# Mask and relative-position bias: from identity matmuls on TensorE to float32 additions in PSUM on VectorE

## The reference

```python
# layer 0, FoX: 16 heads of 128
s = einsum('bqhd,bkhd->bhqk', q, k) * scale
s = s + c[:, :, q0:kl, None] - c[:, :, None, :kl]      # forget-gate prefix sums
s = where(mask, s, -inf); p = softmax(s)
out = einsum('bhqk,bkhd->bqhd', p, v)

# layer 1, differential: 8 heads, two 128-wide q/k maps, 256-wide values
s = einsum('bqhmd,bkhmd->bhmqk', q, k) * scale
s = s + table[t5_bucket(qpos - kpos)]                  # bias by distance, constant from 128 on
s = where(mask, s, -inf); p = softmax(s)
a = p[:, :, 0] - lam * p[:, :, 1]
out = einsum('bhqk,bkhe->bqhe', a, v)                  # then per-head RMSNorm and gain
```

## Time and profile before

| | |
|---|---|
| time, median of 3 runs | 3136.53 us (3135.52 to 3137.95) |
| profiled execution, its own time | 3144.5 us |
| its span on the slowest core (core 4) | 3142.9 us |
| spans of the 8 cores | 3125.1 to 3142.9 us |
| mean granted TensorE clock, each core | 0.982 to 0.984 |
| busy: TensorE, ScalarE, VectorE, GpSimd | 94%, 37%, 33%, 4% |
| fox attention, units 0 to 6; unit 7 | 161 to 1183 us; 1183 to 1246 |
| first epilogue; layer 1's first projections | to about 1530; to 1666 |
| differential attention, units 0 to 6; unit 7 | 1666 to 2818; 2818 to 2890 |

### The profile page before, as it was taken

How to read it: one execution, slowest core, us unless ns; L and a number is a source line. 1 busy time by engine, 2 the same in 40 slices (tenths; PEclk the granted TensorE clock), 3 DMA queues, 4 the chain that set the end, 5 groups by cost and what they waited for, 6 DMA issues and landing times.

```text
span 3142.9 us, 63295 instructions; the slowest of 8 cores (3125.1 to 3142.9 us)
## 1 busy us (share of the span) xinstructions
PE 2968.9 (94%) x22516; PEld 2026.0 (64%) x22516; DVE 1027.2 (33%) x2722; ACT 1178.2 (37%) x2720; POOL 117.2 (4%) x239
## 2 busy tenths in 40 slices
PE   5999999999999996989599999999999999987998
PEld 2758686777768583434266867777777777665443
DVE  0122222222222222454213343434343333335455
ACT  0144554545454447222103333434343333245111
POOL 1000000000000000000000000000000000000000
PEclk9999999999999999999799999999999999999999
DMA  9222111112111119678621111111111111043565
GB/s 151 41 38 45 37 37 35 37 33 48 36 36 33 36 20 167 178 197 210 107 41 35 33 36 31 36 29 29 31 35 35 35 35 33 20 75 92 168 187 172
DMA packets 172112, 212.91 MB, mean 68 GB/s; under 512 B 105344, under 2 KB 150176, under 8 KB 155296
## 3 DMA queue, kind: packets, MB, share of 16 engines
q0 software_dynamic: 22944, 92.41, 17.6%
q1 hardware_dynamic: 148864, 116.47, 13.8%
HBM read 224.19 MB, written 51.90 MB: 88 GB/s over the span
## 4 chain that ended last, share of the span: by engine, by line
PE 84%; DMA 6%; DVE 3%; ACT 3%; issue 2%; SPq 1%; POOL 0%; DVEq 0%; ACTq 0%; POOLq 0%
PE pb L470 29%; PE pb L448 27%; PE pb L622 12%; PE pb L753 8%; PE pb L592 7%; DMA B<-M 3%; PE pb L595 2%; DMA W<-w_in 1%; ACT M L609 1%; DVE E L784 1%; DVE E L782 1%; ACT M L773 1%; DMA escr<-M 1%; ACT M L790 1%; SPq L791 1%
## 5 line engine op out<-in xcount | busy, mean ns | idle before, releaser
L609 ACT ACTIVATE M<-pb,L 128x256 bf16<-128x256 f32 (+1 forms) x1152 | 508.2, 460 | 468.0 <-PE pb L592 345.9
L613 ACT ACTIVATE M<-pb 128x256 bf16<-128x256 f32 (+1 forms) x1152 | 418.9, 371 | 680.4 <-PE pb L592 423.4
L448 PE MATMUL pb<-B,W 128*128 128x512 bf16 x2048 | 513.8, 380 | 35.5 <-ACT A L457 34.5
L448 PE MATMUL pb<-A,W 128*128 128x512 bf16 x2048 | 520.1, 382 | 21.4 <-DMA A<-x_t 21.4
L470 PE MATMUL pb<-W,A 128*128 128x256 bf16 x4096 | 524.3, 274 | 12.5 <-DMA W<-w_in 11.1
L470 PE MATMUL pb<-W,B 128*128 128x256 bf16 x4096 | 517.3, 273 | 0.0
L470 PEld LDWEIGHTS pb<-W,A 128*128 128x128 bf16 x4096 | 399.0, 98 | 57.1 <-issue 13.7
L622 PE MATMUL pb<-A,M 128*128 128x257 bf16 x2176 | 421.8, 274 | 12.3 <-DVE rin L656 6.7
L470 PEld LDWEIGHTS pb<-W,B 128*128 128x128 bf16 x4096 | 396.8, 98 | 45.2
L622 PE MATMUL pb<-B,M 128*128 128x129 bf16 x2176 | 307.4, 221 | 8.8 <-ACT M L609 4.0
L592 PE MATMUL pb<-B 128*128 128x256 bf16 (+1 forms) x1152 | 302.0, 267 | 13.7 <-ACT M L609 13.7
(11 more groups left out here) (87 smaller groups left out, 1854.0 us busy)
## 6 DMA issues: line engine op xcount, KB each, us to landing
W<-w_in POOLq DMA_DIRECT2D x61, 1024.0 KB, 8.5
gd<-M SPq DMA_DIRECT2D x128, 128.0 KB, 1.8
E<-x SPq DMA_DIRECT2D x16, 1024.0 KB, 6.6
x1d<-E SPq DMA_DIRECT2D x16, 1024.0 KB, 4.9
E<-x1d SPq DMA_DIRECT2D x16, 1024.0 KB, 6.4
y<-E SPq DMA_DIRECT2D x16, 1024.0 KB, 4.1
A<-w_out POOLq DMA_DIRECT2D x4, 2048.0 KB, 35.5
B<-w_out POOLq DMA_DIRECT2D x4, 2048.0 KB, 35.2
```

The source lines that it names most:

```text
L448: ins = e.matmul(pb[bk][:, :], lhsT=W[slot][:, kc, m * 128:(m + 1) * 128], rhs=Xbuf[:, kc, tc * 512:(tc + 1) * 512], start=(kc == 0), stop ...
L609: P.op("act", lambda e: e.activation(out=Pt[s][:, 0:w], in_=src, func=AF.Exp, bias=bsel[:, m, j, 2 * I:2 * I + 1], scale=SCALE), reads=rPB ...
L613: P.op("act", lambda e: e.activation(out=Pt[s][:, 0:w], in_=src, func=AF.Exp, scale=SCALE), reads=rPB(bank), writes=r_Pt(s, 0, w))
```

## The change

The identity, its table and its matmuls go. `nmask` and the bias table `Bt` are float32, the two bias blocks of a head side by side (distance 0, then distance 1). `qk` records a single score matmul, and for a diagonal tile one `tensor_tensor` on VectorE that adds the table to the score bank in place; the exponential then reads the bank. That is 32 additions in a fox unit (128 columns) and 46 in a differential one (30 of 128 columns, 16 of 256, j = 2I taking both bias blocks at once). In `setup_head_b` three VectorE operations a head take the place of six.

```diff
-        ident = sb("ident", [128, 128], BF16)
         tri_bf = sb("tri_bf", [128, 128], BF16)
-        nmask_bf = sb("nmask_bf", [128, 128], BF16)
+        nmask = sb("nmask", [128, 128], F32)
...
-                Bt = L[:, 0:4096].rearrange("p (h k l q) -> p h k l q", h=8, k=2, l=2)
+                Bt = L[:, 0:4096].bitcast(F32).rearrange("p (h w) -> p h w", h=8)
...
-                P.op("dve", lambda e: e.tensor_tensor(out=etmp[:, 0, :], in0=etmp[:, 0, :], in1=nmask_bf[:], op=ALU.add),
-                     reads=r0 + rS("nmask_bf"), writes=r0)
-                for k, rk in ((0, r0), (1, r1)):
-                    base = (h * 4 + k * 2) * 128
-                    P.op("dve", lambda e, k=k: e.tensor_copy(out=Bt[:, h, k, 0, :], in_=etmp[:, k, :]),
-                         reads=rk, writes=rL(base, base + 128))
-                    P.op("dve", lambda e, k=k: e.tensor_tensor(out=Bt[:, h, k, 1, :], in0=etmp[:, k, :], in1=Bt[:, h, k, 0, :], op=ALU.subtract),
-                         reads=rk + rL(base, base + 128), writes=rL(base + 128, base + 256))
+                P.op("dve", lambda e: e.tensor_tensor(out=Bt[:, h, 0:128], in0=etmp[:, 0, :], in1=nmask[:], op=ALU.add),
+                     reads=r0 + rS("nmask"), writes=rL(h * 512, h * 512 + 256))
+                P.op("dve", lambda e: e.tensor_copy(out=Bt[:, h, 128:256], in_=etmp[:, 1, :]), reads=r1, writes=rL(h * 512 + 256, h * 512 + 512))
...
-                    extra = []
-                    for k in range(nblk):
-                        d = i0 + k - j
-                        if fox and d == 0:
-                            extra.append((k, nmask_bf[:], rS("nmask_bf")))
-                        elif (not fox) and d in (0, 1):
-                            for l in range(2):
-                                base = (u * 4 + d * 2 + l) * 128
-                                extra.append((k, Bt[:, u, d, l, :], rL(base, base + 128)))
-                    def g(e):
-                        ins = e.matmul(pb[bank][:, 0:w], lhsT=o.k[:, m, j * 128:(j + 1) * 128], rhs=o.q[:, m, q0:q0 + w],
-                                       start=True, stop=(len(extra) == 0))
-                        for n, (k, rhs, _) in enumerate(extra):
-                            ins = e.matmul(pb[bank][:, k * 128:(k + 1) * 128], lhsT=ident[:], rhs=rhs, start=False, stop=(n == len(extra) - 1))
-                        return ins
...
+                    P.op("pe", lambda e: e.matmul(pb[bank][:, 0:w], lhsT=o.k[:, m, j * 128:(j + 1) * 128], rhs=o.q[:, m, q0:q0 + w],
+                                                  start=True, stop=True),
+                         reads=o.rk(m, j * 128, (j + 1) * 128) + o.rq(m, q0, q0 + w), writes=rPB(bank), sig=True)
+                    if fox:
+                        if j < 2 * I:
+                            return
+                        hi, add, r_add = 128, nmask[:], rS("nmask")
+                    else:
+                        if j < 2 * I - 1:
+                            return
+                        d0 = 0 if j >= 2 * I else 1
+                        hi = 256 if j == 2 * I else 128
+                        add = Bt[:, u, d0 * 128:d0 * 128 + hi]
+                        r_add = rL(u * 512 + d0 * 256, u * 512 + d0 * 256 + 2 * hi)
+                    P.op("dve", lambda e: e.tensor_tensor(out=pb[bank][:, 0:hi], in0=pb[bank][:, 0:hi], in1=add, op=ALU.add),
+                         reads=r_add, writes=rPB(bank))
```

More of the change, by code:

```diff
@@ L241, in build_program @@
         r_xres = [rng("E", 4096 + k * 4096, 8192 + k * 4096) for k in range(2)]
-        P.dma("pool", "c0", lambda e: e.dma_start(out=ident[:], in_=consts[:, 0:128]), writes=rS("ident"))
         P.dma("pool", "c1", lambda e: e.dma_start(out=tri_bf[:], in_=consts[:, 128:256]), writes=rS("tri_bf"))
         P.op("pool", lambda e: e.memset(lnst[:, 10:12], -0.5), writes=rS("lnst", 10, 12))
-        P.op("dve", lambda e: e.tensor_scalar(out=nmask_bf[:], in0=tri_bf[:], scalar1=-1.0, scalar2=BIG, op0=ALU.add, op1=ALU.mult),
-             reads=rS("tri_bf"), writes=rS("nmask_bf"))
+        P.op("dve", lambda e: e.tensor_scalar(out=nmask[:], in0=tri_bf[:], scalar1=-1.0, scalar2=BIG, op0=ALU.add, op1=ALU.mult),
+             reads=rS("tri_bf"), writes=rS("nmask"))
         wtile = {"next": 0}
```

## The result

| | before | after |
|---|---|---|
| time, median of 4 runs each | 3137.2 us (3135.5 to 3141.1) | 3214.6 us (3210.6 to 3219.9) |
| ratio | | 1.0246, 95% interval 1.0228 to 1.0264 |
| slowest core's span in the profiled execution | 3142.9 us (core 4) | 3214.1 us (core 0) |
| mean granted clock, each core | 0.982 to 0.984 | 0.968 to 0.970 |
| fox stage, first score matmul to last value matmul | 1081.8 us | 1096.6 us |

What follows compares the result with a forecast made beforehand. TensorE, busy 94% of the span, was taken as the bound, with VectorE's runs deciding the new waits. -62 + 42 + 41 + 4 + 25 + 15 + 30 = +95 us on 3136.5 gave 3232, range 3172 to 3282.

Steps and rivals of the forecast that it cites:

- A: Differential unit changes: first additions stand behind closing, GpSimd and output step; 6.9 us six times, 0.9 at unit 0, 42.
- B: Differential blocks 0 and 1 behind a unit's start: waits of 2.1, 2.2 and 1.6 us, seven times, 41 us.
- Removed: 1,248 identity matmuls gone; 1,092 in units 0 to 6 at 57 ns save 62 us, unit 7's count nothing.
- C: Tail of differential unit 6, without projections and with two banks: four diagonal groups at about 0.9 us, 4 us.
- D: Differential unit 7, where VectorE's runs cover three times as many tiles: waits at entry and in its blocks, 25 us.
- E: Fox layer: unit changes 0.8 us longer seven times (6), unit 7 (6), tail and collisions (3), together 15 us.
- tail and collisions: Small remaining fox losses outside the unit changes and unit 7, put at 3 us.
- F: Granted clock halved behind new waits: differential changes 6 x 2, fox 6 x 1.5, unit 7 5, blocks 0 and 1 4; 30 us.
- Waits without the clock: Rival: 2 us waits leave the clock up, unit 7's four banks hide half its losses; +45, 3182 us, chance 0.24.
- Hidden, faster: Rival: every addition gets VectorE within the 1.2 us slack per tile, only -62 remains; 3074 us, chance 0.04.
- Deeper: Rival: PSUM additions 60 ns longer, half clock at more waits, TensorE setting unit 7; +30, 3262 us, chance 0.14.
- Even: Rival: new waits and saving cancel, runs delaying only each front's first wait; within 6 us of 3137, chance 0.03.

Runs made afterwards that it cites:

- e1_none: The changed kernel with its VectorE additions left out, so no mask and no bias at all; ratio to before 0.9816.
- e4_late: The changed kernel, with the output step of a unit's last block not flushed at the unit change but deferred five iterations; 3202.75 us, ratio to before 1.0195.
- e6_unit7: The changed kernel with identity matmuls instead of VectorE additions in unit 7 of both layers; 3187.3 and 3187.6 us.
- e5_hybrid: The changed kernel with VectorE additions only in blocks where VectorE is free, identity matmuls elsewhere, unit 7 included; ratio to before 0.9898.
- e7_both: The kernel before with all identity matmuls kept, plus the changed kernel's 624 VectorE additions, of zeros; ratio to before 1.0372.
- e2_fox_only: The changed kernel with VectorE additions in the fox layer only, identity matmuls in the differential layer; ratio to before 1.0019.

## Why the forecast held, and where its terms were off

The mechanism is the one forecast: TensorE waits at each front of diagonal tiles behind a closing or an output step, in units 0 to 5 nothing above 0.21 us behind tile 17, and clock beside it. In units 1 to 5 a differential unit takes some 170.3 us against 157.7 in e1_none (distance of first score matmuls): 12.6, where A, B and the clock made 14.8. The two largest misses have opposite signs, the saving 7 us too large and B 15 us too large, so that the total is nearer than its terms.

| term | forecast | measured |
|---|---|---|
| removed | -62 | -55 (e1_none, stages) |
| differential layer: A 42, B 41, C 4, D 25, clock 12 + 4 + 3 | 131 | 113 |
| fox: E 15, clock 9 + 2 | 26 | 27 |
| sum | 95 | 84 in the stages; 77 in the medians |

**Removed** was 7 us too large, and not by its price: 56 ns an identity is what differential unit 0 and the fox units of e1_none show, against 57. The term left out that TensorE, coming sooner, meets the closing of map 0 at five changes (1.06 each) and at unit 7 (5.02 for 4.44). The Trainium skill's figure for such a stream (TensorE: Matmul & The Clock Gate, Back-to-back issue gap), 81 ns, would make it 88 us, an estimate; e1_none, 55 in the stages and 58 with 13 on either side in the time, speaks against it.

**A** held: 6.68 to 7.03 at five changes against 6.9, 5.81 at unit 6, and 0.74 at unit 0 against 0.9: 40.3. e4_late shows that the run ahead of the additions makes it.

**B** was the largest error in size: 41 forecast, 25.6 measured. Its three waits were to be 2.1, 2.2 and 1.6; they are 1.57, 1.47 and 1.01, 4.1 a unit against 5.9. The chain from VectorE free to matmul was right (1.11 us against 1.1). What failed is "Map 1 of block 0 is closed from 4.85 (its last value matmul)", and the tile times beside it. The accumulator of the first 128 queries is complete one iteration before, and its closing starts at 1842.06, 0.39 ahead of the last value matmul at 1842.45; it lasts 3.45 and not 3.1; and without its wait tile 8 would have come 2.60 behind that value matmul (1846.62 - 1.57 - 1842.45), where the forecast had 6.98 - 4.85 = 2.13. From 3.1 + 1.1 - 2.1 = 2.1 it became -0.4 + 3.45 + 1.1 - 2.6 = 1.6. And "seven times" was wrong for unit 6: more than one projection piece lies in each iteration there, tiles come later, and the waits of B are 0.63 and 0.68. Units 0 to 5 make 24.3, unit 6 makes 1.3.

**C** held: eleven waits of 0.18 to 1.21 in unit 6's tail, 4.5 together, where e1_none has four of 1.2 together: 3.3 against 4. **D** held: 27 by e6_unit7, of which some is clock (25, and about 3 of the 5 for unit 7). TensorE's first wait there, 4.44 in the earlier trace rows, became 7.03; 4.4 + 2.3 was forecast. Read singly, A 40.3, B 25.6, C 3.3, D 27 and the clock 14 (below) make 110; from them go the 7.3 that e1_none itself waits at the five changes (1.06 and 0.40 each), and 3.0 come on, by which unit 7 of e6_unit7 is longer than e1_none's. That leaves some 7 of the layer's 113 unplaced, about 1 a unit.

**E** was right in its sum, and its parts were not. Change waits are 2.48 against 2.5, and unit 7 is 6.2 against 6. But e6_unit7's fox stage, with identities in unit 7, is still 20.5 us over e1_none's: 4 are the changes (2.48 for 1.82 at five), 6 the clock, and some 10 are small losses at diagonals. In unit 4, whose clock stays up, they are five, of 0.18 to 0.27 us, all in or next to an iteration without a projection piece, as between two score matmuls at 325.93 and 327.15 in unit 1, 1.22 us where before has 1.09. The forecast had "tail and collisions: 3". The clock paid part back: 4 drops at six changes, since unit 6's wait is only 1.61 and one of 2.48 dropped nothing; 6 us instead of 9. e5_hybrid has 188 of these additions and no longer waits at a change than before, and its stage is 9.5 us over e1_none's, of which its 36 remaining identities are 2: the small losses without the large ones.

**F** was half right. Every differential change drops the clock. At the first it is back at about 1840, 3.8 us behind the end of the wait, at the others 4.2 to 5.4 us behind it; half of that is lost, 1.9 to 2.7 each and 14 together, against 12. No wait of B does: the 4 us for them did not come. The rival *Waits without the clock* (3182) falls with these rows, and it left out half of D, which e6_unit7 shows in full. *Hidden, faster* falls with 3214.6 against e1_none's 3082: the additions are nearly hidden where VectorE is free (e5_hybrid) and nowhere else. *Deeper* falls on its 60 ns, which were at most 7, and *Even* with the time. The experiments' rival, a price for each addition wherever it stands, falls too: 624 of them cost 140 us over e1_none in the stages, and by that price e5_hybrid's 386 would cost 87; its stages are 30.5 over e1_none's, and 19 of these are the 376 identities that it keeps in units 0 to 6, at 51 ns. That leaves 11 us, 30 ns an addition, where VectorE is free.

What stays open: the 84 us of the stages and the 77 of the medians differ by 7 us, and for fox alone by 8. The part between the stages takes it up on the slowest cores (423 us before, 408 after); on the median core of each profiled execution it is 406 and 403. Why it varies from core to core was not tried. And no experiment keeps the waits and leaves out the drops of the clock: its share rests on the times at half speed read from the traces, and what decides whether a wait of some 2.4 us drops it stays open.

## What to carry to other kernels

An engine that is 33% busy has room only where its program order has room: before moving work onto it, find what stands ahead of each new operation in its queue, and compare that run with the slack of the engine behind it. If a saving and a new wait come at the same place, the saving is partly spent inside the wait; and a saving can uncover a wait that was hidden before, as 56 ns an identity became 51. Once the costs are known by place, moving the work only where the queue is empty gave -32 us where moving all of it gave +77. The same view of the queue then showed waits that had been there before the change: 10.5 us in the differential stage and 12 in fox, some 20 in the time.

## What the runs showed of the hardware

- The clock behind a wait is not set by the wait's length alone. At fox changes with waits of 2.48 us it stood at 0.50 behind four and at 1.00 behind the one at 751.62. On all eight cores: behind the 40 waits of 1.71 (before) and the 40 of 1.82 (e1_none) it never fell; behind 2.36 (e7_both) it fell 4 times of 40, behind 2.48 (after) 35 of 40, behind 3.30 (e4_late) and 6.68 every time. Waits of 1.47 to 1.57 in the differential units of after did nothing, but of e4_late's 40 of 2.03 three were followed by a drop, and before's wait of 1.9 at the start of fox unit 7 by matmuls at half speed. A drop cost a fox unit 1.5 us (in e2_fox_only 147.1 us between first score matmuls with one, 145.6 without).
- An in-place float32 `tensor_tensor` in PSUM, with its second operand in SBUF, took 286 to 300 ns for 128 columns (mean 297) and 429 for 256, within 7 ns of one with both in SBUF. The Trainium skill (VectorE: DVE Perf Modes, the section on the TRN2 errata) gives (N+151)/0.96 ns for a float32 addition, an estimate of 291 and 424; these means are 2% and 1% above it.
- Halving a wait from 6.68 to 3.30 us kept most of the loss of clock behind it: 0.50 just behind either, 3.1 to 3.7 us of it behind each of e4_late's changes against 3.8 to 5.4, 10 us lost in all against 14.
